# Moving the heavy expert's down product behind half an up product and a turn, in an fp32 mixture-of-experts kernel

## The reference

```python
logits = (hf @ router).astype(jnp.float32)
top_v, top_i = lax.top_k(logits, TOP_K)
...
for e in range(N_EXPERTS):
    y = y + gates[:, e:e + 1] * swiglu(hf, w_gate[e], w_up[e], w_down[e])
```

## Time and profile before

| | |
|---|---|
| time, median of 3 runs (lowest to highest) | 1854.62 us (1851.88 to 1855.22) |
| the profiled execution's own time | 1850.28 us |
| its span | 1848.4 us |
| TensorE busy / mean granted clock over the span | 1633.0 us (88%) / 0.933 |
| VectorE, ScalarE busy | 1320.4 us (71%), 845.4 us (46%) |
| HBM read, mean rate | 389.30 MB, 211 GB/s |

### The profile page before, as it was taken

How to read it: one execution, slowest core, us unless ns; L and a number is a source line. 1 busy time by engine, 2 the same in 40 slices (tenths; PEclk the granted TensorE clock), 3 DMA queues, 4 the chain that set the end, 5 groups by cost and what they waited for, 6 DMA issues and landing times.

```text
span 1848.4 us, 21405 instructions
## 1 busy us (share of the span) xinstructions
PE 1633.0 (88%) x8461; PEld 1348.3 (73%) x8462; DVE 1320.4 (71%) x1449; ACT 845.4 (46%) x826; POOL 0.2 (0%) x4
## 2 busy tenths in 40 slices
PE   4988899999999696997699999988888889889885
PEld 1876687888887596566678887877777777777773
DVE  5858757777777727673588989876577668668676
ACT  5421322221221434332467776755465548557564
POOL 0000000000000000000000000000000000000000
PEclk8988999999999897898799999999989889999898
DMA  9544333543675220000799999987679769879873
GB/s 352 189 158 138 113 110 127 174 158 117 222 237 177 63 92 1 1 1 18 255 321 335 355 345 323 365 284 257 207 281 334 250 200 348 275 255 378 282 256 123
DMA packets 209452, 391.80 MB, mean 212 GB/s; under 512 B 7818, under 2 KB 82220, under 8 KB 209348
## 3 DMA queue, kind: packets, MB, share of 16 engines
q1 hardware_dynamic: 204826, 385.77, 60.2%
q10 hardware_dynamic: 4522, 4.61, 0.8%
HBM read 389.30 MB, written 1.05 MB: 211 GB/s over the span
## 4 chain that ended last, share of the span: by engine, by line
PE 75%; DVE 13%; ACT 6%; issue 3%; DMA 1%; SPq 1%; DVEq 0%; ACTq 0%
PE bank L563 19%; PE bank L565 19%; PE bank L564 18%; DVE lo L522 7%; ACT hi L516 4%; PE bank L2111 2%; PE bank L2089 2%; PE bank L1991 2%; PE bank L2127 2%; PE bank L1980 2%; PE bank L2090 2%; PE bank L2128 2%; PE bank L1766 1%; PE bank L1997 1%; DMA raw<-in_ada_w_dram 1%
## 5 line engine op out<-in xcount | busy, mean ns | idle before, releaser
L522 DVE TENSOR_TENSOR lo<-raw,hi 128x2048 fp32r<-128x2048 f32 x328 | 742.9, 2279 | 299.4 <-ACT hi L516 298.9
L516 ACT ACTIVATE hi<-raw 128x2048 fp32r<-128x2048 f32 x328 | 622.7, 1907 | 565.5 <-PE bank L565 472.9
L2089 PE MATMUL bank<-hi,xg 128*128 128x512 f32 (+1 forms) x384 | 152.7, 403 | 14.3 <-DVE lo L522 7.4
L2090 PE MATMUL bank<-lo,xg 128*128 128x512 f32 (+1 forms) x384 | 149.1, 394 | 0.0
L1178 DVE SCALAR_TENSOR_TENSOR acc<-raw,cs,acc 128x512 f32<-128x512 f32 x216 | 146.5, 745 | 1.4
L563 PE MATMUL bank<-Hhi,hi 128*128 128x512 f32 x352 | 141.1, 401 | 2.8 <-issue 2.8
L565 PE MATMUL bank<-Hhi,lo 128*128 128x512 f32 x352 | 139.4, 396 | 0.0
L564 PE MATMUL bank<-Hlo,hi 128*128 128x512 f32 x352 | 138.4, 393 | 0.0
L563 PE MATMUL bank<-H3h,hi 128*128 128x256 f32 x352 | 101.6, 289 | 11.4 <-DVE lo L522 11.4
L563 PE MATMUL bank<-hi,xg 128*128 128x512 f32 (+1 forms) x288 | 109.2, 379 | 1.1 <-ACT xg L936 0.8
L564 PE MATMUL bank<-lo,xg 128*128 128x512 f32 (+1 forms) x288 | 108.0, 375 | 0.0
(11 more groups left out here) (366 smaller groups left out, 3109.5 us busy)
## 6 DMA issues: line engine op xcount, KB each, us to landing
raw<-in_moe_w_gate_dram SPq DMA_DIRECT2D x88, 1024.0 KB, 6.2
raw<-in_moe_w_up_dram SPq DMA_DIRECT2D x88, 1024.0 KB, 5.9
raw<-in_moe_w_down_dram SPq DMA_DIRECT2D x88, 1024.0 KB, 5.4
raw<-in_ada_w_dram SPq DMA_DIRECT2D x48, 1024.0 KB, 5.6
raw<-in_ffn_w_gate_dram SPq DMA_DIRECT2D x11, 1024.0 KB, 5.4
raw<-in_ffn_w_up_dram SPq DMA_DIRECT2D x11, 1024.0 KB, 5.4
raw<-in_ffn_w_down_dram SPq DMA_DIRECT2D x11, 1024.0 KB, 5.0
raw<-in_ab_w_in_dram SPq DMA_DIRECT2D x6, 1024.0 KB, 8.7
```

The source lines that it names most:

```text
L516: nc.scalar.activation(hi[n0 % SPL][:, 0:size], raw[slot][:, 0:size], ACT.Copy).then_inc(hi_ready, 1)
L522: nc.vector.tensor_tensor(lo[n0 % SPL][:, 0:size], raw[slot][:, 0:size], hi[n0 % SPL][:, 0:size].bitcast(F32), ALU.subtract).then_inc(lo_r ...
L2089: T.matmul(b[:, 0:n_], xg[:, kk, 0:P], wh[:, k, :], start=(kk == 0), stop=False, skip_group_check=True)
L2090: ins = T.matmul(b[:, 0:n_], xg[:, kk, FEW:FEW + P], wl[:, k, :], start=False, stop=(kk == KD - 1), skip_group_check=True)
```

## The change

In `moe_slabs` and on TensorE the order of a heavy chunk becomes `hg hu g0 g1 u0, turn(c - 1), hd, u1`; the turn now stands behind u0 in every chunk of experts 1 to 7, heavy or not. On ScalarE, `heavy_hi` goes from one position behind to hu's own, and on VectorE `heavy_product` goes ahead of the position's split and `heavy_lo` right behind it. `few_gate`, `few_hi`, `few_product` and `few_lo` follow the turn (a new helper `turned_by` names the slab behind which a chunk is turned). hd's four sums go to banks 6, 7, 4 + c % 2 and 5 - c % 2, the last of which is the bank of the turn just ahead. TensorE enters expert 4 with `zeroed` >= 1, and waits for 2 ahead of its down product. The router's small loads are issued ahead of the last norm.

```diff
@@ moe_slabs
             order += [(w, first_slab("g", c) + q) for q in range(parts)]
+            order += [(w, first_slab("u", c))]
             order += [("hd", n)] if n is not None else []
-            order += [(w, first_slab("u", c) + q) for q in range(parts)]
+            order += [(w, first_slab("u", c) + q) for q in range(1, parts)]
@@ bank_order
+        return [(("hd", n, o), (6, 7, 4 + c % 2, 5 - c % 2)[o]) + ((("hd", n),) if o == 3 else ()) for o in range(4)]
...
-            moe += heavy_out(n) if n is not None else []
             moe.append((("u", w, c), 2 + c % 2, (w, last_slab("u", c))))
+            moe += [(("t", w, c - 1), 4 + (c - 1) % 2)] if c else []
+            moe += heavy_out(n, c) if n is not None else []
@@ new helper
+        def turned_by(s):
+            return 5 if s == 24 else next((c - 1 for c in range(1, 6) if s == first_slab("u", c)), None)
@@ ScalarE, before the mixture
-            roots(3, x_ready[2])
-            norm(3, 1, 2)
             for dst, src in ((router[:], a["moe_router"][0].rearrange("(k p) e -> p k e", p=P)), (tri, a["k_tri"]),
...
             act.dma_start(fgain[:], a["final_gain"].partition_broadcast(P)).then_inc(fgain_in, 16)
+            roots(3, x_ready[2])
+            norm(3, 1, 2)
@@ ScalarE, position p
+                if w == "hu":
+                    heavy_hi(s)
...
-                if back(p, 1)[0] == "hu":
-                    heavy_hi(back(p, 1)[1])
...
+                if w in LIGHT and CAPS[w] == FEW and turned_by(s) is not None:
+                    few_gate(w, turned_by(s))
                 w, s = back(p, 1)
...
+                if w in LIGHT and CAPS[w] == FEW and turned_by(s) is not None:
+                    few_hi(w, turned_by(s))
@@ VectorE, position p
-                if p < len(MOE):
-                    split_lo(dve, "moe", MOE[p])
                 w, s = back(p)
                 if w == "hu":
                     heavy_product(s)
-                if back(p, 1)[0] == "hu":
-                    heavy_lo(back(p, 1)[1])
+                if p < len(MOE):
+                    split_lo(dve, "moe", MOE[p])
+                if w == "hu":
+                    heavy_lo(s)
...
+                if w in LIGHT and CAPS[w] == FEW and turned_by(s) is not None:
+                    few_product(w, turned_by(s))
                 w, s = back(p, 1)
...
+                if w in LIGHT and CAPS[w] == FEW and turned_by(s) is not None:
+                    few_lo(w, turned_by(s))
@@ TensorE
                         if w == 4:
-                            pe.wait_ge(zeroed, 2)
-                    for kind in "gu":
...
+                            pe.wait_ge(zeroed, 1)
+                    parts = 2 if c < 5 else 1
+                    for kind, only in (("g", range(parts)), ("u", range(1)), ("u", range(1, parts))):
+                        if few and only:
+                            few_features(kind, w, c, only)
+                        elif only:
+                            features("moe", kind, w, c, only=only)
+                        if (kind, only) != ("u", range(1)):
+                            continue
+                        if c and few:
+                            few_turn(w, c - 1)
+                        elif c:
+                            turn("moe", w, c - 1)
+                        if n is not None:
                             heavy_down(n)
...
-                    if c and few:
-                        few_turn(w, c - 1)
-                    elif c:
-                        turn("moe", w, c - 1)
+                if w == 4:
+                    pe.wait_ge(zeroed, 2)
                 down_e("moe", w)
```

More of the change, by code:

```diff
@@ L194, in heavy_in, with heavy_out @@
         return [(("hg", n), c % 2, ("hg", n)), (("hu", n), 2 + c % 2, ("hu", n))]
-    def heavy_out(n):
-        return [(("hd", n, o), 4 + o) + ((("hd", n),) if o == 3 else ()) for o in range(4)]
+    def heavy_out(n, c):
+        return [(("hd", n, o), (6, 7, 4 + c % 2, 5 - c % 2)[o]) + ((("hd", n),) if o == 3 else ()) for o in range(4)]
     moe = []
@@ L205, in bank_order @@
             moe.append((("g", w, c), c % 2, (w, last_slab("g", c))))
-            moe += heavy_out(n) if n is not None else []
             moe.append((("u", w, c), 2 + c % 2, (w, last_slab("u", c))))
+            moe += [(("t", w, c - 1), 4 + (c - 1) % 2)] if c else []
+            moe += heavy_out(n, c) if n is not None else []
             moe += scatter(w - 1) if c == 0 and w > 1 else []
-            moe += [(("t", w, c - 1), 4 + (c - 1) % 2)] if c else []
         moe += [(("d", w, 0), 6), (("d", w, 1), 7, (w, 32)), (("t", w, 5), 5)]
@@ L2063, in gather_places, with features @@
                 filled(ins, stage, ("pt", w))
-            def features(st, kind, w, c, it=0):
+            def features(st, kind, w, c, it=0, only=None):
                 n_ = 512 if c < 5 else 256
@@ L2069, in features @@
                 parts = 2 if c < 5 else 1
-                for q in range(parts):
+                for q in range(parts) if only is None else only:
                     blocks = KD // parts
@@ L2077, in features, with few_features @@
                     used(ins)
-            def few_features(kind, w, c):
+            def few_features(kind, w, c, only):
                 n_ = 512 if c < 5 else 256
@@ L2083, in few_features @@
                 parts = 2 if c < 5 else 1
-                for q in range(parts):
+                for q in only:
                     blocks = KD // parts
@@ L2215, in _ @@
                         if w == 4:
-                            pe.wait_ge(zeroed, 2)
-                    for kind in "gu":
-                        if few:
-                            few_features(kind, w, c)
-                        else:
-                            features("moe", kind, w, c)
-                        if kind == "g" and n is not None:
+                            pe.wait_ge(zeroed, 1)
[12 more added lines that the diff above has]
+                        if n is not None:
                             heavy_down(n)
```

## The result

| | before | after |
|---|---|---|
| time, median (lowest to highest) | 1854.92 us (1851.88 to 1864.92, 4 runs) | 1785.76 us (1783.81 to 1789.57, 4 runs) |
| ratio, 95% interval | | 0.9637 (0.9610 to 0.9664) |
| profiled execution, own time / span | 1850.28 / 1848.4 us | 1786.58 / 1784.8 us |
| mean granted clock over the span | 0.933 | 0.950 |

The changed kernel is 3.6% faster, and the forecast of 1788.5 us lies 2.7 us above its median.

A forecast was written before the change was run, and what follows sets the result against it. TensorE, busy 88%, was taken as the bound, its heavy-chunk waits and slow clock to win. Terms 17.0 + 10.4 + 16.0 + 12.8 - 4.7 + 1.7 + 6.0 + 6.8 = 66.0 us; 1850.3 to 1784.3, plus 4.3: 1788.5 us, range 1774 to 1812.

The forecast's parts named there:

- The walk: Step-by-step times of a heavy chunk after the change, at full clock; hd starts at 8.2 us without a wait.
- Y: Second slab behind u1 in a heavy chunk, held by hd's buffer, ready at 18.4 us; TensorE waits 0.8 us.
- Z: Third slab behind u1 in a heavy chunk, ready at 22.4 us behind two additions; TensorE waits about 2 us.
- four groups: Ten heavy chunks: heavy behind heavy 17.0 us, light chunk behind 10.4, at c = 1 16.0, at c = 4 12.8.
- The clock: Slow clock behind new waits in the ten heavy chunks gives back 4.7 us; bounds 0 and -16.
- Chunk 0 and expert 4's entry: Heavy chunk 0 loses its 2.19 us wait, gain 1.7; expert 4's entry loses a 6.54 us wait, gain 6.0.
- The router: Small loads ahead of the norm save 4.0 us of waiting; matmuls meeting full clock save 2.8; together 6.8 us.
- Loads: Rival, few experts: loads become the bound because shorter heavy chunks leave buffers unfilled; 22 us lost, 1811 us; 12%.
- Half of it stays: Rival, heavy chunks: VectorE a slab late, each chunk waits some 3 us more; 30 us lost, 1818 us; 9%.
- The heavy wait stays: Rival: hd still waits as long for hal, only router and expert 4's entry count, 12.8 us; 1842 us; 3%.
- hal: Low part of the heavy product, which hd needs; predicted made by VectorE at 5.1 us, before hd's start at 8.2.
- Slower by the clock: Rival: several short waits drop TensorE to 1.2 GHz, up to 13 us more per heavy chunk; 1914 us; 3%.

The follow-up runs named there:

- early_adds: The changed kernel with all four additions of a heavy chunk ahead of the split at position hd; 1763.63 us, ratio 0.9520.
- changed_again: The changed kernel itself, run again on the same chip as no_order; 1785.40 us, ratio 0.9629.
- router_only: The kernel before with only the router's seven small loads issued ahead of the last norm; 1850.26 us, ratio 0.9984.
- old_banks: The changed kernel with hd's four sums in banks 4 to 7 again; 1830.71 us, ratio 0.9874.
- parts_only: The kernel before with only the places of heavy product, high part and low part changed; 1795.97 us, ratio 0.9698.
- order_only: The changed kernel with heavy product, high part and low part back at their old places; 1790.41 us, ratio 0.9664.
- old_order_best: The kernel before, its slab order, turn and banks kept, with moved parts, early additions, early router loads and expert 4's early entry; 1755.40 us, ratio 0.9485.
- no_order: The changed kernel with slab order, turn and banks as in the kernel before; 1790.23 us, ratio 0.9655.
- early_adds_again: The same kernel as early_adds, run once more on another chip beside old_order_best; 1763.89 us, ratio 0.9521.
- zeroed_only: The kernel before with only expert 4 entered behind zeroed >= 1 and its down product behind 2; 1848.19 us, ratio 0.9971.

## Why the prediction was right

**What bounds it.** Right: TensorE's waits in the heavy chunks and the clock behind them were the time to win. The mechanism was right, and most terms were; that the total came as near as 2.7 us is in part luck, as the clock and the scatter below show.

**The walk.** In (4,1) TensorE was predicted to start the turn at 6.4, hd at 8.2 and the next hg at 29.65 behind hu's end (33.66 less 4.0). It did at 6.60, 8.30 and 29.15, and hd took 5.7 us at c = 3, where 5.6 were predicted. u0's wait was predicted as 0.8 and is 0.76; hd's wait for the last sum's bank at c = 1 was predicted as 1.2 and is 0.68; Y's 0.8 and 0.66; Z's about 2 and 1.81; the turn's at c = 4 about 2.9 and 2.46. (4,3) was to take 27.0 and took 27.14; (4,4) 25.0 and 24.91. hg to hg from (4,1) to (4,3) took 40.45 us, where 40 were predicted. Each of the four groups came within 1 us of its term, 56.2 us predicted and 56.1 measured; but the terms were for full clock, and the measured gains have the clock's loss in them.

**The clock.** I took off another 4.7 us. In after, five stretches at half clock begin in the heavy chunks, from 1477.67 to 1726.85, together 20.5 us long, of which the last 3.7 us of the first lie in expert 5's down product. What they cost is read from like chunks with and without one: (6,1) and (7,1) take 30.58 us, (4,1) and (5,1) 29.15; (5,4) takes 26.15 and (4,4) 24.91. So it is some 1.4 us each, some 7 us for the five, and the term was too small by some 2.3 us. At full clock the ten chunks would thus have gained some 63 us instead of 56.2. Of these 7 us more some 2 are (4,1)'s walk, which ends 0.5 us early in each of four chunks, some 2 are (6,3) and (7,3), and some 3 are chunks of before that I had not taken as samples and that ran slower than these: (5,3) took 36.42 us where (4,3) took 35.56, and (7,1) 34.67 where (4,1) took 33.66. Nine of the ten had a second slow stretch, behind the turn's wait, where in the heavy chunk read first I had named only hd's. This row of the kernel before, behind the turn of (4,3), shows it:

```profile
1322.55:1324.67 2.12, 2.12 (x11) 2.12 (x11) 2.12 (x4) 0.00 (x0) 0.00 (x0) 0.50 0.76 240
```

The two errors don't cancel quite: less the clock I had 51.5 us for the ten chunks, and they brought 56.1. Chunk 0 brought 1.2 us more than its term and the router 2.2 less, which makes 69.6 instead of 66.0; the 6.9 us that came out longer elsewhere more than took that back, and nothing in the prediction foresaw them. early_adds shows what the whole is worth: with no wait above 1.5 us left behind expert 4's entry, there is no slow stretch in the few experts.

**Chunk 0 and expert 4's entry.** 1.7 predicted, 2.2 measured without the clock in hg and hu; 6.0 and 6.0, with the two waits foreseen as 2.9 us together measured as 0.76 + 2.09.

**The router: the step that failed.** 4.0 us for the wait was right in kind: 3.8. The 2.8 us for the clock was wrong in this execution, since all 32 matmuls ran at the slow pace (6.97 us, as before the change), although the same 5.86 us of idleness and the same 16 transposes stood ahead of them. I had read one full-clock stretch of 3.4 us in one execution as a property of the kernel. It differs between executions of one kernel: the changed kernel has the slow form in after and the fast one in changed_again, and early_adds has the slow one where its repeat has the fast one. Four of the nine executions with the loads ahead of the norm have the fast form, which saves 2.5 us, so its mean is 1.1 us and the term 3.8 + 1.1, and router_only's ±3.3 us can't confirm even that. The Trainium skill, "TensorE: Matmul & The Clock Gate", Part 4, says that transposes don't raise the clock. By it no execution should be fast: five of the nine agree with it, and four don't, so it doesn't hold here as it stands. Against this one result, 4.6 us, its 4.0 was nearer than my 6.8.

**The rivals.** *Loads:* ScalarE's waits for them went from 7.5 us to 6.8; fallen. *Half of it stays:* hd's wait for its last sum is 0.68 at c = 1 and nothing at c = 3; fallen, but old_banks shows that the place was rightly named, since with other banks it is 3.72 to 5.02 us at c = 3 and c = 1 and costs 44 us in all. *The heavy wait stays:* fallen; hal has 3.2 us to spare. *Slower by the clock:* fallen, since all its waits of 0.7 to 2.5 us cost some 7 us of clock together, where the rival took up to 13 in each of ten chunks.

**What I didn't ask.** The prediction priced the whole and was near, but it didn't say which part of the change pays. The experiments do. By ratios against 1855 us, and less 8 us for the two small edits where a kernel has them (3.0 and 5.4 us, each ± 3), the heavy chunks gain, in us:

| order, turn | banks | parts early | kernel | gain |
|---|---|---|---|---|
| | | x | parts_only | 56 |
| x | x | | order_only | 54 |
| x | | x | old_banks | 15 |
| x | x | x | after | 59 |

I can't show from this what the order with the old banks and the old parts would do; it wasn't tried.

## What to carry to other kernels

Where a stalled consumer waits for a chain of small steps on in-order engines, try first to move these steps ahead of the long ones that stand before them (here two lines on VectorE and one on ScalarE brought 56 of 59 us), and only then the order of the large work, which can just exchange one wait for another, as the banks of old_banks did, and which cost 5 us here once the rest was right (old_order_best). After such a change look for the idle time that is left on the engine that feeds the bound one: moving the additions into VectorE's 3.77 us brought 22 us more. And price a clock effect from several executions, since one shows only what happened once.

## What the runs showed of the hardware

In the few experts waits of 3.7 to 6.5 us of TensorE (eleven in before, eight in old_banks) each had a stretch at the 1.2 GHz level at their end or within 1.2 us behind it, and 3.0 to 5.9 us of it lay behind the wait. The thirty waits of 1.26 us for hal in parts_only, no_order and old_order_best had no slow stretch right behind them, and early_adds kept 1.00 for 515 us with waits of up to 1.5 us. But a short wait is no surety elsewhere: in chunk 0 TensorE waits 1.08 us for ScalarE's gathered copies ahead of g0, and right behind that the clock stayed at 1.00 in after and fell in changed_again, early_adds_again, old_banks and old_order_best. The row of changed_again is

```profile
910.70:914.05 3.35, 3.22 (x8) 2.57 (x9) 0.23 (x1) 0.03 (x1) 0.00 (x0) 0.50 1.00 326
```

From 1.4 to 2.5 us the runs show both. Z's wait of 1.81 us comes six times in after, always ahead of the same work: two times the clock stayed at 1.00 and four times it fell, as the rows at 1267.87 and 1682.30 in the section on the result show. Which chunks they are differs between after and changed_again. A wait of 2.00 to 2.11 us at expert 4's entry left the clock alone in after and was followed by a slow stretch in early_adds, early_adds_again and old_order_best, whose row is

```profile
1225.23:1228.60 3.37, 3.37 (x10) 2.65 (x9) 3.37 (x2) 0.51 (x1) 0.00 (x0) 0.51 0.82 261
```

The executions also scatter ahead of all this work. The norm's transposes, which stand behind the first 860 us of the program, started between 862.4 and 866.8 us in the twelve profiled executions, although the kernels don't differ ahead of that point but in where the seven small loads are issued, and 862.4 (old_order_best) and 866.8 (no_order) both come with them early, 863.0 (parts_only) and 866.0 (zeroed_only) with them late. So a difference of 4 us between two single profiles must be read stretch by stretch.
